# One decoder program on one core: raw rows turned for the first router, half of the expert sum on TensorE, layer norm from sums made in the projection, all convolution chunks on GpSimd

## The reference

```python
def first_block(x, ...):
    # attention over 256 context and 512 own tokens, and a retention scan, give mix
    x = x + mod[:, 2] * (mix @ w_out[l])                       # "out1"
    hf = modulate(rms_norm(x, g_ffn[l]), mod[:, 3], mod[:, 4])
    x = x + mod[:, 5] * moe_ffn(hf, ...)                       # 32 experts, top 4
    return x

def moe_ffn(h, w_router, b_router, w1, b1, w2, b2):
    logits = h @ w_router + b_router
    top_val, top_idx = lax.top_k(logits, TOP_K)
    gates = jax.nn.softmax(top_val, axis=-1)
    # each token: sum over its 4 experts of gate * (act(h @ w1[e] + b1[e]) @ w2[e] + b2[e])

def second_block(x, ...):
    # latent_mixer: input projection; a 5-tap convolution of 12 * 128 channels along the tokens,
    # then a state-space scan; beside it attention of 16 heads over 256 + 512 keys; w_out ("out2")
    x = layer_norm(alpha * x + g_a * latent_mixer(...), ln1_g[l], ln1_b[l])
    x = layer_norm(alpha * x + g_f * hier_moe(x * (1.0 + sc_f) + sh_f, p), ln2_g[l], ln2_b[l])

def layer_norm(x, g, b, eps=1e-5):
    mu = jnp.mean(x, -1, keepdims=True)
    var = jnp.mean(jnp.square(x - mu), -1, keepdims=True)
    return (x - mu) * lax.rsqrt(var + eps) * g + b
```

## Time and profile before

| | |
|---|---|
| median of 3 runs | 2644.3 us (2641.42 to 2649.74) |
| profiled execution | 2643.12 us |
| its span, first to last instruction | 2641.3 us |
| mean granted PE clock | 0.891 |
| PE busy | 2162.1 us (82%) |
| DVE busy | 1044.6 us (40%) |
| ACT busy | 736.8 us (28%) |
| POOL busy | 255.9 us (10%) |

### The profile page before, as it was taken

How to read it: one execution, slowest core, us unless ns; L and a number is a source line. 1 busy time by engine, 2 the same in 40 slices (tenths; PEclk the granted TensorE clock), 3 DMA queues, 4 the chain that set the end, 5 groups by cost and what they waited for, 6 DMA issues and landing times. The chain is left out here.

```text
span 2641.3 us, 43783 instructions
## 1 busy us (share of the span) xinstructions
PE 2162.1 (82%) x18060; PEld 1223.0 (46%) x18060; DVE 1044.6 (40%) x1992; ACT 736.8 (28%) x1868; POOL 255.9 (10%) x219
## 2 busy tenths in 40 slices
PE   3989779749998998888889886599979976693895
PEld 2965256633333343333333332488856634572442
DVE  2235455442222222222222222646167678434343
ACT  3223445221111110111111110244156658411222
POOL 0000000000000000000000001100089540000001
PEclk8999889959999899998998997799989995795897
DMA  6356710238999999999999996522000011301995
GB/s 221 112 197 235 283 55 1 74 143 337 421 421 420 415 420 421 421 422 422 421 421 421 421 421 251 169 80 96 1 1 1 1 65 64 136 5 59 417 418 201
DMA packets 147195, 628.03 MB, mean 238 GB/s; under 512 B 34420, under 2 KB 65396, under 8 KB 93240
## 3 DMA queue, kind: packets, MB, share of 16 engines
q1 hardware_dynamic: 118728, 579.76, 54.2%
q0 software_dynamic: 8064, 29.36, 2.9%
q10 hardware_dynamic: 20208, 16.15, 1.9%
HBM read 591.85 MB, written 33.38 MB: 237 GB/s over the span
## 5 line engine op out<-in xcount | busy, mean ns | idle before, releaser
L2156 PE MATMUL psum<-w,x 128*32 128x512 f32 x5184 | 622.0, 628 | 112.7 <-DMA w<-in_w_mlp 103.7
L2156 PEld LDWEIGHTS psum<-w,x 128*32 128x32 f32 x5184 | 163.7, 113 | 511.0 <-issue 340.2
L2316 DVE TENSOR_TENSOR u<-psum,x 128x512 f32<-128x512 f32 x81 | 56.0, 692 | 715.9 <-PE psum L2156 715.9
L739 PE MATMUL psum<-high 128*128 128x512 f32 (+3 forms) x832 | 293.0, 352 | 38.2 <-DVE low L761 38.2
L2165 PE MATMUL psum<-w,act_turned 128*32 128x256 f32 x5184 | 299.9, 384 | 4.3 <-DMA w<-in_w_mlp 4.0
L739 PE MATMUL psum<-high,low 128*128 128x512 f32 (+3 forms) x832 | 292.2, 351 | 0.0
L739 PE MATMUL psum<-low,high 128*128 128x512 f32 (+3 forms) x832 | 292.0, 351 | 0.0
L2165 PEld LDWEIGHTS psum<-w,act_turned 128*32 128x32 f32 x5184 | 168.9, 112 | 164.1 <-issue 66.3
L761 DVE TENSOR_TENSOR low<-weight_slots,high 128x1024 fp32r<-128x1024 f32 (+3 forms) x84 | 89.3, 1067 | 262.2 <-ACT high L755 261.7
L739 PEld LDWEIGHTS psum<-high 128*128 128x128 f32 x832 | 159.1, 191 | 60.8 <-ACT high L755 37.7
L2257 ACT ACTIVATE sig<-glu 128x256 f32<-128x256 f32 x81 | 34.5, 426 | 485.1 <-DVE glu L2317 485.0
(11 more groups left out here) (503 smaller groups left out, 2809.7 us busy)
## 6 DMA issues: line engine op xcount, KB each, us to landing
w<-in_w_mlp SPq DMA_DIRECT2D x192, 2048.0 KB, 28.4
weight_slots<-in_w_ada SPq DMA_DIRECT2D x12, 2048.0 KB, 11.0
weight_slots<-in_w_mod SPq DMA_DIRECT2D x12, 2048.0 KB, 10.9
weight_slots<-in_w_in SPq DMA_DIRECT2D x9, 2048.0 KB, 8.9
gu<-in_w_gate SPq DMA_DIRECT2D x16, 1024.0 KB, 29.3
gu<-in_w_up SPq DMA_DIRECT2D x16, 1024.0 KB, 31.4
down<-in_w_down SPq DMA_DIRECT2D x16, 1024.0 KB, 30.6
weight_slots<-in_w_out SPq DMA_DIRECT2D x6, 2048.0 KB, 11.4
```

The costliest lines, as they stand in the source:

```text
L739: mm = pe.matmul(psum[:, p.group % 8, 0:p.width], *p.operands(x, weights[:, n % 2], u * QK_ + kc, kc), start=p.first and u == 0 and kc == ...
L2156: mm = pe.matmul(psum[g * RB:(g + 1) * RB, bank, :], b.turned[:, kc, q * RB:(q + 1) * RB], w[:, i, g * BANK:(g + 1) * BANK], start=kc == 0 ...
L2316: step.reach(dve.tensor_tensor(b.u[:], psum[:, bank, :], b.bias[:], ALU.add), s.biased, at + 1)
```

## The change

Four places change.

1. First router. `norm_rows` goes. `turn_raw` has PE turn the raw `k.x` at once, while ACT squares the tiles; DVE takes out six banks and ACT two, with the scale alone. `logits_of_raw` multiplies these un-normed features by the router and applies each row's rate to the logits; the shift's part of the logits is a product with ones. The normed rows are made there, two tiles by ACT and two by DVE, and stored from ACT's queue. SP's waits for that store stand in `places_by_rank` now. The second router keeps `to_features` and `logits_of`, with the router's loads ahead of the rows' store, whose wait has moved as well.
2. `combine`: all 16 gathers have their own buffer; choices 0 and 1 of a tile are summed on PE behind the bias, with identity tiles weighted by ACT; DVE adds choices 2 and 3.
3. `layer_norm`: the row sums come from the `accum_out` of out2's L1738; gain and bias are loaded during out2 into a weight slot that has come free; ACT takes the squares with the mean as bias, and each tile goes through on its own.
4. `attn2`: POOL takes all 12 chunks of the convolution; `convolve` goes.

The diff, cut to its core:

```diff
@@ attention
-                for c in range((DS + SG * SN) // P):
+                for c in range(DXBC // P):
...
-                    if t == 2 and 1 <= head <= conv_ops:
-                        convolve(head - 1)
@@ project_out
             return dve.scalar_tensor_tensor(out=k.x[:, t, cols], in0=k.x[:, t, cols], scalar=alpha, in1=bank,
-                                            op0=ALU.mult, op1=ALU.add)
+                                            op0=ALU.mult, op1=ALU.add,
+                                            **({"accum_out": k.x_sums[:, n, t:t + 1]} if norm else {}))
@@ places_by_rank, SP
+            sync.wait_ge(k.rows_stored, stored)
+            sync.wait_ge(k.slots_cleared, 16)
@@
+def turn_raw(core, k, name, b, prefetch, x_rows):
+    by_scalar = (2, 5)
...
+        def _(pe):
+            for m in range(DC):
+                for t in range(TX):
+                    mm = pe.transpose(psum[:, m, t * P:(t + 1) * P], k.x[:, t, m * P:(m + 1) * P], k.ident[:])
+                mm.then_inc(s.turned, 1)
...
+        def _(act):
+            act.dma_start(x_rows.rearrange("(t p) d -> p t d", p=P), k.x[:]).then_inc(k.x_stored, 16)
+            act.activation(c.warm[:], k.eps[:, 0:1], ACT.Sqrt).then_inc(s.warmed, 1)
+            for t in range(TX):
...
+                act.activation(c.junk[:], k.x[:, t], ACT.Square, accum_out=c.sums[:, t:t + 1]).then_inc(s.squared, 1)
+                if t >= 2:
+                    keep(act, by_scalar[t - 2])
+            act.wait_ge(s.squared, TX)
+            act.activation(c.roots[:], c.sums[:], ACT.Sqrt, scale=1.0 / D, bias=k.eps[:, 0:1]).then_inc(s.rooted, 1)
...
+def logits_of_raw(core, k, name, b, r, width, loaded, xn, rows):
...
+            mm.then_inc(s.summed, 1)
+            pe.wait_ge(s.shift_summed, 1)
+            pe.matmul(psum[:, 2, 0:width], k.ones[:], c.products_sum[:], start=True, stop=True).then_inc(s.offset_summed, 1)
+            pe.wait_ge(s.kept, 1)
...
+            act.copy(c.partial[:], psum[:, 0, :]).then_inc(s.kept, 1)
+            act.wait_ge(s.xn_made, TX)
+            store_rows(k, xn[:], rows)(act)
...
+            for t in range(by_scalar, TX):
+                scaled_rows(dve, t)
+            dve.wait_ge(s.offset_summed, 1)
+            step(dve.tensor_tensor(c.offset[:], psum[:, 2, 0:width], b.bias[:], ALU.add))
+            dve.wait_ge(s.joined, 1)
+            for t in range(TX):
+                step.later(dve.scalar_tensor_tensor(out=r.logits[:, t], in0=psum[:, 1, t * 32:(t + 1) * 32],
+                                                    scalar=b.rates[:, t:t + 1], in1=c.offset[:], op0=ALU.mult, op1=ALU.add))
@@ store_rows
-        if others:
-            others(engine)
-        engine.wait_ge(k.rows_stored, 16 * which)
-        engine.wait_ge(k.slots_cleared, 16)
@@ combine
-    ahead = 4
+    by_tensor = top // 2
...
+            sync.dma_start(b.bias[:], bias).then_inc(s.bias_loaded, 16)
             sync.dma_start(b.gate[:], on_all(rows[0:1, 5 * D:6 * D])).then_inc(s.gate_loaded, 16)
+            for t in range(TX):
+                sync.dma_start(k.x[:, t], x_rows[t * P:(t + 1) * P, :]).then_inc(x_loaded[t], 16)
...
-                if i >= ahead:
-                    pool.wait_ge(s.added, i - ahead + 1)
...
+                for j in range(by_tensor):
                     for c in range(D // BANK):
...
+                        mm = pe.matmul(sums_ps[:, t, c * BANK:(c + 1) * BANK], b.shares[:, t, j],
+                                       b.got[:, t, j, c * BANK:(c + 1) * BANK], start=False, stop=j == by_tensor - 1)
+                mm.then_inc(s.summed, 1)
...
+                    ins = act.activation(b.shares[:, t, j], k.ident[:], ACT.Copy, scale=r.gates[:, t, j:j + 1])
...
+                dve.wait_ge(s.summed, t + 1)
+                dve.wait_ge(rest[t], 16 * (top - by_tensor))
+                for j in range(by_tensor, top):
+                    step(dve.scalar_tensor_tensor(out=total, in0=b.got[:, t, j], scalar=r.gates[:, t, j:j + 1],
+                                                  in1=sums_ps[:, t] if j == by_tensor else total, op0=ALU.mult, op1=ALU.add))
@@ expert_layer, second router
+                def before(engine):
+                    load(engine)
+                    store_rows(k, k.x[:], rows)(engine)
@@ layer_norm
-def layer_norm(core, k, name, gain, bias):
+def layer_norm(core, k, name, loaded_rows):
...
+            act.wait_ge(s.averaged, 1)
             for t in range(TX):
...
+                act.activation(b.junk[:], k.x[:, t], ACT.Square, bias=b.means[:, t:t + 1],
+                               accum_out=b.squares[:, t:t + 1]).then_inc(s.squared, 1)
...
+            def centre(t):
+                step.later(dve.scalar_tensor_tensor(out=b.scaled[:, t % 2], in0=k.x[:, t], scalar=b.means[:, t:t + 1],
+                                                    in1=gain, op0=ALU.add, op1=ALU.mult))
+
+            def finish(t):
+                dve.wait_ge(s.rooted, t + 1)
+                step(dve.reciprocal(b.rates[:, t:t + 1], b.roots[:, t:t + 1]))
+                dve.scalar_tensor_tensor(out=k.x[:, t], in0=b.scaled[:, t % 2], scalar=b.rates[:, t:t + 1], in1=bias,
+                                         op0=ALU.mult, op1=ALU.add).then_inc(s.finished, 1)
```

More of the change, by code:

```diff
@@ L456, in _ @@
             dve.wait_ge(s.vector_step, step.count)
[L459 to L482, removed]
 def to_features(core, k, name, groups, prefetch=None):
@@ L1708, in first_mixer, with project_out @@
         project_out(core, k, "out1", lambda t, i: m.mix[:, t, i * P:(i + 1) * P], MIX1, args.w_out[0], k.rows1, 1.0)
-def project_out(core, k, name, mix, width, w_out, rows, alpha, gain=None):
+def project_out(core, k, name, mix, width, w_out, rows, alpha, gain=None, norm=None):
     kc = width // P
@@ L2683, in _, with combine @@
                 dve.tensor_tensor(b.y[:, 0, 0], psum[:, 2, 0:YW], b.gate[:], ALU.mult).then_inc(s.y_kept, 1)
-def combine(core, k, name, r, y_rows, rows, top, alpha, bias=None, x_rows=None):
-    ahead = 4
+def combine(core, k, name, r, y_rows, rows, top, bias, x_rows):
     psum = core.psum
-    experts = 0 if bias is None else bias.shape[0]
-    more = {} if bias is None else {"bias": [experts, D], "spread_turned": [experts, L]}
-    with buffers(core, got=[P, ahead, D], total=[P, D], gate=[P, D], **more) as b, \
+    experts = bias.shape[0]
+    by_tensor = top // 2
+    with buffers(core, got=[P, TX, top, D], total=[P, 2, D], gate=[P, D], bias=[experts, D], spread_turned=[experts, L],
+                 shares=[P, TX, by_tensor, P]) as b, \
             stage(core, name, "gate_loaded", "added", "vector_step", "bias_loaded", "shares_turned", "shares_kept",
-                  "biased", *[f"x{t}_loaded" for t in range(TX)], pool_dma=("got0", "got1", "got2", "got3")) as (block, s):
-        got = [s.got0, s.got1, s.got2, s.got3]
-        work = [(t, j) for t in range(TX) for j in range(top)]
-        bias_ps = psum[:, :, :].rearrange("p (t c) n -> p t (c n)", t=TX)
+                  "spread_out", "summed", *[f"x{t}_loaded" for t in range(TX)],
+                  pool_dma=("first0", "first1", "first2", "first3", "rest0", "rest1", "rest2", "rest3")) as (block, s):
+        first = [s.first0, s.first1, s.first2, s.first3]
+        rest = [s.rest0, s.rest1, s.rest2, s.rest3]
+        sums_ps = psum[:, :, :].rearrange("p (t c) n -> p t (c n)", t=TX)
         x_loaded = [s.x0_loaded, s.x1_loaded, s.x2_loaded, s.x3_loaded]
@@ L2739, in _ @@
+        @block.scalar
+        def _(act):
+            act.wait_ge(s.shares_turned, 1)
+            act.copy(b.spread_turned[:], psum[0:experts, 7, :]).then_inc(s.shares_kept, 1)
+            for t in range(TX):
+                for j in range(by_tensor):
+                    ins = act.activation(b.shares[:, t, j], k.ident[:], ACT.Copy, scale=r.gates[:, t, j:j + 1])
+                ins.then_inc(s.spread_out, 1)
+            act.wait_ge(s.spread_out, TX)
         @block.vector
@@ L2912 @@
 SPAN = WIDE - TAPS + 1
-def layer_norm(core, k, name, gain, bias):
-    with buffers(core, sums=[P, TX], squares=[P, TX], roots=[P, TX], rates=[P, TX], eps=[P, 1], junk=[P, D],
-                 gain=[P, D], bias=[P, D]) as b, \
-            stage(core, name, "loaded", "summed", "centred", "rooted", "scalar_step", "vector_step", "eps_set") \
+def layer_norm(core, k, name, loaded_rows):
+    gain, bias = loaded_rows[:, 0:D], loaded_rows[:, D:2 * D]
+    with buffers(core, sums=[P, TX], means=[P, TX], squares=[P, TX], roots=[P, TX], rates=[P, TX], eps=[P, 1], warm=[P, 1],
+                 junk=[P, D], scaled=[P, 2, D]) as b, \
+            stage(core, name, "eps_set", "warmed", "averaged", "squared", "rooted", "finished", "vector_step") \
             as (block, s):
-        @block.sync
-        def _(sync):
-            sync.dma_start(b.gain[:], on_all(gain)).then_inc(s.loaded, 16)
-            sync.dma_start(b.bias[:], on_all(bias)).then_inc(s.loaded, 16)
         @block.gpsimd
```

243 lines of the change are left out of this document (137 added, 106 removed).

## The result

The changed kernel took 2605.5 us, the median of four runs (2603.19 to 2615.03), against 2646.1 for the kernel before (four runs): a ratio of 0.9846, 95% interval 0.9824 to 0.9867. The forecast was 2608 in a range of 2600 to 2624. In a second timing four runs of the same program had a median of 2609.1, nine of the kernel before 2646.7: ratio 0.9853, interval 0.9838 to 0.9868. The span of the profiled execution is 2601.3 us, 40.0 less than before.

A forecast was written before the change was run, and what follows sets the result against it. The long middle was taken as bound by streaming expert weights, which the change leaves alone; gains outside it, 7.0 + 4.0 + 9.6 + 9.0 + 5.7 = 35.3 us, taken from 2643.1 gave 2607.8, forecast as 2608, range 2600 to 2624.

The forecast's parts named there:

- First router: From the projection's end to the first choice: a gain of 7.0 us, from 5.5 to 9.2.
- The chain through ACT: First router: ACT's table load, squares and evictions end last; with allowances and stage change, logits matmuls start at 535.7.
- so I take the slow one: First router: after some 3 us idle on PE, the logits matmuls take 3.64 us, not 1.92.
- the fast branch: First router: with fast matmuls and joins the choice starts at 540.8, a gain of 9.2 us.
- Second router: Router's loads ahead of the rows' store: no bias wait, faster matmuls and joins; 4.0 us gained, from 0 to 4.6.
- First combine: Sixteen gathers without waits, clock rising in tile 0's sums, tile 3's last gathers ending the wait: 9.6 us gained.
- The rival of a clock at 0.50 throughout: First combine: PE stays at 1.2 GHz, stage 4.2 us worse instead of 9.6 better, total 2621.6; chance 0.14.
- Layer norm: After out2: row sums from evictions, eight full-width DVE operations, 11.3 us long; 9.0 us gained, down to 8.0.
- Attention: Second attention: all convolution chunks on POOL, DVE loses ten operations; 5.7 us gained, POOL ending just ahead.
- some 1.0 of each hides in DVE's waits: Second attention: of each long convolution operation 1.0 us is hidden; the rest, 8 × 0.7 = 5.6 us, is on the path.
- the rival of POOL as the bound: Second attention: POOL outlasts attention at 15.83 us a chunk, gain 1.5 instead of 5.7, total 2612.0; chance 0.10.
- The serial gathers: First combine: each gather waits for the one before to land, 103 us in all, total 2679; chance 0.04.

The follow-up runs named there:

- store-first run: Changed kernel with the second router's rows stored ahead of the router's loads, still without that stage's wait: first turn to bias addition 15.6 us.
- the run without the split: Changed kernel keeping the first combine's sixteen buffers, but VectorE adds all four shares and TensorE does only the biases: stage 46.4 us.
- the run with extra turns: Changed kernel with 24 unused identity turns on TensorE ahead of tile 0's sums in the first combine: stage 40.3 us.

## Why the prediction was right, and where its terms were off

The total came closer than its terms. They were short by 2 to 5 us, but the base of the sum, 2643.1, lies 3.0 under the median of the kernel before, 2646.1; the two errors cancel in part, and that is luck.

- *First router, 7.0 forecast, 9.27 measured.* The chain through ACT was right as an order, but it was not what ended last. The matmuls begin 9.6 us after the projection (forecast 535.7 − 526.0 = 9.7), and that they agree is luck: ACT's chain with the stage change was over after 9.04, less than allowed, and then the matmuls waited 0.57 for the router's bias, a wait that the sum doesn't have. With the store of x on SP they begin after 8.6, and no bias is waited for. The step that failed by more is "so I take the slow one". The matmuls and joins ran at the upper clock, 5.14 us from the matmuls' start to the choice in this trace and 5.1 to 5.2 in the others, the one with the wait put back aside, where the fast branch had 5.1. The bound of 9.2 that the text gave for that branch is what came.
- *The stores' waits.* Cost nothing in the ranking, as forecast: the first gather of the experts comes 29.66 us after the choice, 29.68 before.
- *Second router, 4.0 and 5.10.* The mechanism held (the order alone, by the store-first run), and the faster matmuls with it. That it came out above the bound of 4.6 is mostly the turns, 0.76 us faster than before, which the sum left as they were: the granted clock rose 3.0 us into them instead of 4.6. Why it rose sooner stays open.
- *First combine, 9.6 and 9.15 (6.5 to 9.15 over eight traces).* The level of the clock decided, as said, and it rose within tile 0's sums. The number is right, the last wait is not. Not as forecast: "the last two gathers of tile 3 end the wait". PE does, end to end from its first sums, which begin 11.4 us into the stage because the gathers share the queues with x (8.1 without its loads). PE's last sums end 1.9 us after the last gather has landed, so the forecast missed by little. In four of the eight traces the clock rises later, and tile 0's sums take 6.5 to 6.6 us instead of 5.0 to 5.5; that is about half of the stage's spread, and the rest is their start, 11.4 to 12.8 us into the stage. The rival of a clock at 0.50 throughout is out.
- *Layer norm, 9.0 and 8.91.* Its rows took 11.1 us against 11.3 forecast. No run takes this part apart, so which of its steps is worth how much stays argued.
- *Attention, 5.7 and 7.91 (7.2 to 7.9 over the traces with this attention).* The mechanism was right, the size was not: "some 1.0 of each hides in DVE's waits" holds for ordinary heads (11.00 to 10.04, 0.96 of an operation of 1.93), but heads that change keys hide less (15.51 to 14.66 with an operation of 1.24, 15.88 to 14.66 with one of 1.62). A short operation, which the sum put at nothing, stood in such a head as well and was worth 0.8 (15.47 to 14.65). POOL took 15.28 a chunk, as forecast, and ended first by 0.31 us, not by 3: DVE gained more than forecast, and the rival of POOL as the bound missed by that.
- *The serial gathers* of the other side did not come: sixteen deep they moved 408 to 420 GB/s.
- *The clock and the biases.* They left the granted clock at 0.50 again, 14 us of them in the run without the split. The Trainium skill, "TensorE: Matmul & The Clock Gate", Part 1, would have had it rise; the runs say no.
- *The price on POOL.* A chunk costs twice what it did on DVE, and still the move pays, since POOL ends first. The Trainium skill, "GPSIMD Engine Reference", 4.1, has the price right.

## What to carry to other kernels

Splitting work between engines and removing the waits on buffers can each be worth little or less than nothing alone, and much together; try them together before dropping either. Where TensorE is fed by transfers, making it faster or feeding one tile sooner can put it ahead of the next transfer, and the wait costs it the clock. When work goes to an idle engine, its price there matters less than the distance between the two ends, and that distance says how much more can go.

## What the runs showed of the hardware

An idle gap alone does not tell whether TensorE's clock falls: after 3.69 us idle in the first router the matmuls ran at the upper level (granted clock 1.00, 1.92 us), after 1.47 us in the run with extra turns the sums began at the lower (0.50, 5.29 us instead of 3.70). The 24 turns of 128 by 128 in that run raised the granted clock from 0.50 to 1.00, while sixteen bias matmuls with 32 rows, 14 us in a row, did not. And a stage without any change in its code, scan and out2, moved by up to 5.8 us from trace to trace, as much as a term of the sum: a stage's gain is safest read in several traces.
